# The last gate block computed inside the state-space scan

## The reference

```python
zxbcdt = einsum('bld,de->ble', h, w_in)      # z: the gate, 2048 columns
xbc = silu(conv4(xbc)); dt = softplus(dt + dt_bias); a = -exp(a_log)
def step(state, inp):                         # 2 chunks of 128 tokens, 8 groups of 4 heads
    acs = cumsum(dt_c * a, axis=1)
    decay = exp(where(causal, acs[:, :, None] - acs[:, None, :], -inf))
    cb = einsum('bign,bjgn->bijg', c_c, b_c)
    w = cb[..., None] * decay * dt_c[:, None]
    y_diag = einsum('bijgr,bjgrp->bigrp', w, x_c)
    y_off = einsum('bign,bgrpn->bigrp', c_c, state) * exp(acs)[..., None]
    new_state = ...                           # B^T (x * to_end) + decayed state
y = (y + d * x) * silu(z); y = rmsnorm(y) * gate_norm_w; out = y @ w_out
```

## Time and profile before

| what | us |
|---|---|
| median of three runs (lowest, highest) | 1849.14 (1848.16, 1850.11) |
| the profiled execution: its own time | 1850.63 |
| its span | 1849.0 |
| TensorE busy in the span | 1824.6 (99%) |
| VectorE busy | 1497.7 (81%) |
| ScalarE busy | 1267.7 (69%) |
| GpSimd busy | 118.0 (6%) |
| stretch of the last gate block and the scan | 771.03 to 825.50 |

### The profile page before, as it was taken

One profiled execution on the slowest core, in us unless ns is written; L12 is line 12 of the kernel. 1 busy time (PEld: TensorE's weight loads), 2 busy tenths in 40 slices (PEclk: granted clock), 3 DMA queues, 4 the chain that ended last, 5 costly groups with the idle time before them and its releaser, 6 DMA issues.

```text
span 1849.0 us, 27263 instructions
## 1 busy us (share of the span) xinstructions
PE 1824.6 (99%) x9312; PEld 1547.3 (84%) x9312; DVE 1497.7 (81%) x1847; ACT 1267.7 (69%) x1651; POOL 118.0 (6%) x214
## 2 busy tenths in 40 slices
PE   9999999999999999999999999999999999999997
PEld 7888788888888899888888888888888888888886
DVE  6686777777666788585898999999999999999998
ACT  5645565556544576675678778777787787777876
POOL 2040040000000000150100000000000000000100
PEclk9999999999999999999899999999999999999999
DMA  9434568563655455506799999999999999999994
GB/s 327 157 95 138 180 185 327 188 198 115 199 186 176 157 194 183 174 11 204 249 398 351 413 366 375 395 358 402 381 362 405 366 385 377 367 406 372 374 413 177
DMA packets 239355, 512.48 MB, mean 277 GB/s; under 512 B 11004, under 2 KB 58458, under 8 KB 239210
## 3 DMA queue, kind: packets, MB, share of 16 engines
q1 hardware_dynamic: 235490, 493.34, 73.4%
q0 software_dynamic: 3808, 18.38, 2.6%
HBM read 505.38 MB, written 12.07 MB: 280 GB/s over the span
## 4 chain that ended last, share of the span: by engine, by line
PE 93%; DVE 4%; ACT 1%; issue 1%; DMA 0%; ACTq 0%; SPq 0%; DVEq 0%
PE ps L261 24%; PE ps L263 24%; PE ps L262 24%; PE ps L2288 9%; PE ps L2291 4%; PE ps L2549 1%; DVE w_lo L254 1%; PE ps L2426 1%; PE ps L2129 1%; PE ps L2451 1%; ACT w_hi L245 0%; PE ps L2518 0%; PE ps L2529 0%; PE ps L2052 0%; PE ps L2344 0%
## 5 line engine op out<-in xcount | busy, mean ns | idle before, releaser
L254 DVE TENSOR_TENSOR w_lo<-raw,w_hi 128x1024 fp32r<-128x1024 f32 x938 | 1102.4, 1224 | 145.7 <-ACT w_hi L245 145.6
L245 ACT ACTIVATE w_hi<-raw 128x1024 fp32r<-128x1024 f32 x938 | 941.8, 1055 | 256.3 <-PE ps L263 241.0
L261 PE MATMUL ps<-w_hi,a 128*128 128x512 f32 (+1 forms) x1216 | 480.7, 395 | 2.1 <-DVE w_lo L1334 1.0
L263 PE MATMUL ps<-w_hi,a 128*128 128x512 f32 (+1 forms) x1216 | 472.8, 389 | 0.0
L262 PE MATMUL ps<-w_lo,a 128*128 128x512 f32 (+1 forms) x1216 | 471.8, 388 | 0.0
L261 PE MATMUL ps<-w_hi,a_hi 128*128 128x512 f32 (+1 forms) x720 | 280.4, 390 | 1.6 <-DVE a_lo L1905 1.0
L263 PE MATMUL ps<-w_hi,a_lo 128*128 128x512 f32 (+1 forms) x720 | 278.7, 387 | 0.0
L262 PE MATMUL ps<-w_lo,a_hi 128*128 128x512 f32 (+1 forms) x720 | 278.6, 387 | 0.0
L261 PEld LDWEIGHTS ps<-w_hi,a 128*128 128x128 f32 x1216 | 228.5, 188 | 49.6 <-DVE w_lo L254 1.6
L263 PEld LDWEIGHTS ps<-w_hi,a 128*128 128x128 f32 x1216 | 228.3, 188 | 48.0
L262 PEld LDWEIGHTS ps<-w_lo,a 128*128 128x128 f32 x1216 | 228.7, 188 | 44.3
(11 more groups left out here) (362 smaller groups left out, 1452.1 us busy)
## 6 DMA issues: line engine op xcount, KB each, us to landing
raw<-in_moe_w_gate_dram SPq DMA_DIRECT2D x112, 1024.0 KB, 6.9
raw<-in_moe_w_up_dram SPq DMA_DIRECT2D x112, 1024.0 KB, 7.3
raw<-in_moe_w_down_dram SPq DMA_DIRECT2D x112, 1024.0 KB, 7.1
raw<-in_ssd_w_in_dram SPq DMA_DIRECT2D x24, 1024.0 KB, 5.1
raw<-in_w_ffn_in_dram SPq DMA_DIRECT2D x22, 1024.0 KB, 5.0
raw<-in_w_in_dram SPq DMA_DIRECT2D x21, 1024.0 KB, 6.3
raw<-in_w_ffn_out_dram SPq DMA_DIRECT2D x11, 1024.0 KB, 5.0
raw<-in_dense_w_gate_dram SPq DMA_DIRECT2D x11, 1024.0 KB, 5.1
```

The source lines that it names most:

```text
L245: nc.scalar.activation(w_hi[:, u % SPL, part], raw[:, u % RAW, part], ACT.Copy).then_inc(hi_done, 1)
L254: last = nc.vector.tensor_tensor(w_lo[:, u % SPL, part], raw[:, u % RAW, part], w_hi[:, u % SPL, part].bitcast(F32), ALU.subtract)
L261: nc.tensor.matmul(o, lh, rh, start=start, stop=False, skip_group_check=True)
L263: return nc.tensor.matmul(o, ll, rh, start=False, stop=stop, skip_group_check=True)
```

## The change

Four things change.
- The broadcast of the running sums. A third small matmul gives the running sums of both halves and all heads, transposed and twice (rows 0 to 63 and again 64 to 127). VectorE rounds them, leaves the rounding's remainder in the second copy, and spreads them over four blocks, one for each head of a group (`acs_blocks`). A column of ones and zeros (`pick_group`) then picks a group in one rounded matmul of 512 columns.
- Gate block 3 is cut into eight groups of six matmuls (`gate_columns(n)`), the first before the scan's loop, the others in tiles 0 to 6, behind weights(k+2). It uses banks 5 and 6.
- Banks. Outputs of tiles 0 to 9 all use bank 4 and wait for the sum of the tile before; the state shares bank 7 with the carried part and waits for the sum of the last tile.
- Orders. weights(k+2) come before the state. z_out(3) moves behind decays(10), the split of the output unit behind decays(7) on ScalarE and ahead of sum 7 on VectorE.

```diff
@@ setup
+        acs_rows = nc.alloc_sbuf_tensor_at("acs_rows", [P, P], F32R, offset=A1_AT + 4 * 1024)
+        acs_blocks = nc.alloc_sbuf_tensor_at("acs_blocks", [P, HPG, P], F32R, offset=A1_AT + 4 * 512)
+        pick_group = nc.alloc_sbuf_tensor_at("pick_group", [P, 2 * NG], F32R, offset=A1_AT + 4 * 1152)
+        dta_twice = sm[:, 7:9, :].rearrange("p a h -> p (a h)")
+        in_group = stat[:, 8:8 + HPG]
...
-        Z_BANKS = (4, 6, 4, 6)
+        Z_BANKS = (4, 6, 4, 5)
+        ALONE = 10
+        def y_bank(k):
+            return 4 if k < ALONE else 4 + k % 2
@@ ScalarE
-                split_hi(act, O0 + 1)
-                z_out(3)
                 for k in range(2 * NG):
                     if k % 2 == 0:
                         act.wait_ge(st_s, k // 2 + 1)
-                        nc.scalar.activation(s_st, ps[6][:, 0:256].rearrange("p (r e) -> p r e", r=HPG),
+                        nc.scalar.activation(s_st, ps[7][:, 0:256].rearrange("p (r e) -> p r e", r=HPG),
                                              ACT.Copy).then_inc(st_sc, 1)
                     if k + 2 < 2 * NG:
                         decays(k + 2)
+                    if k == 5:
+                        split_hi(act, O0 + 1)
+                    if k == 8:
+                        z_out(3)
@@ VectorE, ahead of the convolution loop
+                nc.vector.tensor_copy(sm[:, 7:9, :], bcast(dta, 1, 2)).then_inc(sd_dta, 1)
...
+                nc.vector.tensor_reduce(in_group, ident.rearrange("p (k r) -> p r k", r=HPG), AX.X, ALU.add)
+                C.link(nc.vector.tensor_reduce(stat[:, 16:32], ident.rearrange("p (a k r) -> p k a r", a=2, r=HPG), AX.XY, ALU.add))
+                nc.vector.tensor_copy(pick_group[:, :], stat[:, 16:32])
@@ VectorE, behind the loop
                 dve.wait_ge(sd_acs, 1)
+                acsT = ps[7][:, P:2 * P]
+                C.link(nc.vector.tensor_copy(acs_rows[:, :], acsT))
+                C.link(nc.vector.tensor_tensor(acs_rows[64:P, :], acsT[64:P, :], acs_rows[64:P, :].bitcast(F32), ALU.subtract))
+                nc.vector.tensor_tensor(acs_blocks[:, :, :], bcast(acs_rows[:, :].bitcast(F32), 1, HPG), bcast(in_group, 2, P),
+                                        ALU.mult)
@@ VectorE, scan
-                split_lo(dve, O0 + 1)
-                dve.wait_ge(zs_done, 4)
+                dve.wait_ge(zs_done, 3)
                 for k in range(2 * NG):
+                    if k == 7:
+                        split_lo(dve, O0 + 1)
+                    if k == 12:
+                        dve.wait_ge(zs_done, 4)
@@ TensorE
-                nc.tensor.matmul(ps[7][:, 64:128], ones, dta, start=True, stop=True).then_inc(sd_acs, 1)
+                nc.tensor.matmul(ps[7][:, 64:128], ones, dta, start=True, stop=True)
+                nc.tensor.matmul(ps[7][:, P:2 * P], dta_twice, upper, start=True, stop=True).then_inc(sd_acs, 1)
...
-                    for r in range(HPG):
-                        hd = t * NH + HPG * g + r
-                        nc.tensor.matmul(ps[k % 2][:, r * P:(r + 1) * P], dta[:, hd:hd + 1].to_broadcast([P, P]), upper,
-                                         start=True, stop=True)
+                    at = NG * t + g
+                    nc.tensor.matmul(ps[k % 2][:, :], pick_group[:, at:at + 1].to_broadcast([P, P]),
+                                     acs_blocks.rearrange("p r i -> p (r i)"), start=True, stop=True)
...
                 def tile_state(g):
                     pe.wait_ge(st_xd, 3 * g + 2)
-                    nc.tensor.matmul(ps[6][:, 0:256], s_b0[:, g, :], s_xe.rearrange("p r e -> p (r e)"),
+                    if g:
+                        pe.wait_ge(st_acc, 2 * g)
+                    nc.tensor.matmul(ps[7][:, 0:256], s_b0[:, g, :], s_xe.rearrange("p r e -> p (r e)"),
...
                     pe.wait_ge(st_w, k + 1)
-                    if k >= 2:
+                    if 0 < k < ALONE:
+                        pe.wait_ge(st_acc, k)
+                    elif k:
                         pe.wait_ge(st_acc, k - 1)
+                    if k == ALONE + 1:
+                        pe.wait_ge(zs_done, 4)
...
+                def gate_columns(n):
+                    half, k = n // 4, n % 4
+                    if k == 0:
+                        pe.wait_ge(lo_done, Z0 + 6 + half + 1)
+                    cols = slice(k * WB, (k + 1) * WB)
+                    for t in range(T):
+                        last = mm3(ps[5 + t][:, :], a0_hi[:, n, t * P:(t + 1) * P], a0_lo[:, n, t * P:(t + 1) * P],
+                                   w_hi[:, (Z0 + 6 + half) % SPL, cols], w_lo[:, (Z0 + 6 + half) % SPL, cols],
+                                   n == 0, n == DC - 1)
+                    if k == 3:
+                        last.then_inc(unit_used, 1)
+
                 tile_weights(0)
                 tile_weights(1)
-                pe.wait_ge(zs_done, 2)
-                mm_rows(pe, Z0 + 6, ps[6:8])
                 pe.wait_ge(zs_done, 3)
+                gate_columns(0)
                 for k in range(2 * NG):
+                    if k + 2 < 2 * NG:
+                        tile_weights(k + 2)
+                    if k + 1 < DC:
+                        gate_columns(k + 1)
                     if k and k % 2 == 0:
                         tile_state(k // 2)
-                    if k + 2 < 2 * NG:
-                        tile_weights(k + 2)
                     tile_output(k)
                     if k == 0:
-                        pe.wait_ge(zs_done, 4)
                         tile_state(0)
```

More of the change, by code:

```diff
@@ L1695, in _ @@
                 C.link(nc.vector.scalar_tensor_tensor(dt, lgt, 0.0, lg2, ALU.max, ALU.add))
-                nc.vector.scalar_tensor_tensor(dta.rearrange("p (t h) -> p t h", t=T),
-                                               dt.rearrange("p (t h) -> p t h", t=T), -1.0, bcast(ea[:, 0:NH], 1, T),
-                                               ALU.mult, ALU.mult).then_inc(sd_dta, 1)
+                C.link(nc.vector.scalar_tensor_tensor(dta.rearrange("p (t h) -> p t h", t=T),
+                                                      dt.rearrange("p (t h) -> p t h", t=T), -1.0, bcast(ea[:, 0:NH], 1, T),
+                                                      ALU.mult, ALU.mult))
+                nc.vector.tensor_copy(sm[:, 7:9, :], bcast(dta, 1, 2)).then_inc(sd_dta, 1)
                 def block_taps(blk):
@@ L1751, in accumulate @@
                         nc.vector.tensor_tensor(before, before, bcast(eacs[:, heads], 2, HD), ALU.mult)
-                    last = nc.vector.tensor_tensor(xv, xv, ps[4 + k % 2][:, 0:256].rearrange("p (r e) -> p r e", r=HPG),
+                    last = nc.vector.tensor_tensor(xv, xv, ps[y_bank(k)][:, 0:256].rearrange("p (r e) -> p r e", r=HPG),
                                                    ALU.add)
@@ L2447, in tile_output @@
                     pe.wait_ge(st_w, k + 1)
-                    if k >= 2:
+                    if 0 < k < ALONE:
+                        pe.wait_ge(st_acc, k)
+                    elif k:
                         pe.wait_ge(st_acc, k - 1)
+                    if k == ALONE + 1:
+                        pe.wait_ge(zs_done, 4)
                     for r in range(HPG):
-                        last = nc.tensor.matmul(ps[4 + k % 2][:, r * HD:(r + 1) * HD], s_ex[k % 3][:, r, :], s_xd[k % 2][:, r, :],
+                        last = nc.tensor.matmul(ps[y_bank(k)][:, r * HD:(r + 1) * HD], s_ex[k % 3][:, r, :], s_xd[k % 2][:, r, :],
                                                 start=True, stop=True)
                     last.then_inc(st_y, 1)
+                def gate_columns(n):
[9 more added lines that the diff above has]
+                        last.then_inc(unit_used, 1)
                 tile_weights(0)
                 tile_weights(1)
-                pe.wait_ge(zs_done, 2)
-                mm_rows(pe, Z0 + 6, ps[6:8])
                 pe.wait_ge(zs_done, 3)
+                gate_columns(0)
                 for k in range(2 * NG):
+                    if k + 2 < 2 * NG:
+                        tile_weights(k + 2)
+                    if k + 1 < DC:
+                        gate_columns(k + 1)
                     if k and k % 2 == 0:
                         tile_state(k // 2)
-                    if k + 2 < 2 * NG:
-                        tile_weights(k + 2)
                     tile_output(k)
                     if k == 0:
-                        pe.wait_ge(zs_done, 4)
                         tile_state(0)
```

## The result

The changed kernel takes 1854.63 us (median of 21 runs, 1849.42 to 1863.82); the kernel before, on the same chip, 1849.14 (21 runs). By the medians it is 5.5 us slower. The ratio is 1.0035, with a 95% interval of 1.0024 to 1.0045, or 6.5 us (4.4 to 8.3). Forecast were 1852.0, in the range 1847.0 to 1856.5. So the sign was right, and the time lies in that range. It lies beyond the 0.2% that I called no change, for which I gave 0.53 (0.37 for slower than that), and beyond the 1850 to 1854 that I gave the forecast's own mechanism.

The account below looks back on a forecast made before the run. TensorE was taken to bound the scan, VectorE close behind. Tiles 0 to 6 -3.5, tiles 7 to 15 +5.1, transposed sum +0.2, slower split +0.4 and clock +0.7 gave +2.9 us: median 1852.0 us, range 1847.0 to 1856.5.

Parts of the forecast that it names:

- the forecast's own mechanism: Whole scan: gain in tiles 0 to 6, larger loss in tiles 7 to 15; 1850 to 1854 us, chance 0.52.
- The broadcast: Scan tiles: weights on TensorE fall from 1.14 to 0.45 us each, 11.0 us less TensorE work, preparation on VectorE hidden.
- TensorE's count: Rival, whole scan: TensorE's work alone sets the time, -6.8 us, 1842.3 us; chance 0.08.
- rival of a costly matmul: Rival, scan broadcast: rounded matmul costs today's price, tiles 0 to 6 take 4.6 us more, 1856.6 us; chance 0.05.
- a bank never late: Rival, tiles 7 to 15: the shared bank delays nobody, VectorE's work sets the end, -2.1 us, 1847.0; chance 0.13.
- Opening: Scan start: TensorE idles 2.4 us for z_out(2), then 1.6 us for the first exp, both released by ScalarE.
- Tiles 7 to 15: Later scan: split, sum 7, state 4, tables, exp 11 in turn; 27.8 us against 22.7, +5.1 us.
- The split beside GpSimd: Output unit's split ahead of sum 7 on VectorE: slower while GpSimd works, 0 to +0.7, taken +0.4 us.
- The tables: ScalarE around z_out(3): two loads of 1.28 us; switch drains, 2.8 us more by the skill page, left out.
- The clock: Opening and tile 8: granted clock falls after TensorE's idle time, bounds 0 and 1.5, taken +0.7 us.
- a clock of 0.50 through several tiles: Sign in the scan that the forecast is wrong: TensorE at half clock over several tiles.
- rival of the low clock: Rival, opening and thin tiles: clock stays low 10 us at each wait, 2 and 2.2 us lost, 1855.5; chance 0.22.

Follow-up runs that it names:

- block_ahead: Changed kernel with all 48 gate matmuls, the split and z_out(3) ahead of the tiles, banks and waits as changed; 1855.50 us.
- held_early2: held_early without the 26 filler transposes ahead of state 4; 1849.24 us.
- held_bank: fillers2 with the carried part in the upper half of its tile's output bank, so no state waits for the sum before; 1849.24 us.
- own_bank: Changed kernel with the carried part in the upper half of its tile's output bank, bank 7 holding the state alone; 1852.03 us.
- fillers: Changed kernel with unread transposes in TensorE's waits in the opening and ahead of states 4 and 7; 1856.09 us.
- fillers2: fillers with 18 more transposes ahead of weights 13, and 10 ahead of each of states 6 and 7; 1851.26 us.
- held_copy: fillers2 with z_out(3) as a plain copy without silu, so ScalarE loads no table inside the scan; 1850.62 us.
- early_split: Changed kernel with the output unit's split earlier: high part behind decays(5), low part ahead of sum 4; 1857.72 us.
- bcast_alone: Kernel before with only the rounded broadcast and its preparation; 1844.68 us.
- held_early: fillers2 with the split's high part behind decays(5) and its low part ahead of sum 4, all fillers kept; 1851.67 us.

## Why the prediction was right, and where it was not

**The broadcast.** A tile's weights take 0.45 us on TensorE with gate columns behind them (798.46 to 798.91), as taken, and 0.54 with the carried part behind them (801.62 to 802.16). The preparation is hidden; ahead of the convolution it is four instructions and not five, 1.07 us together. That TensorE's count doesn't govern is shown twice: alone the edit gives 4.8 of 11.0 us, and pairs stop at 4.40 us, where TensorE waits for VectorE. The rival of a costly matmul falls by these prices, that of a bank never late by the waits of about 1 us ahead of the states in block_ahead and held_early2, and by held_bank.

**Opening.** 2.22 us idle (2.4 laid out), released by ScalarE, then 0.81 instead of 1.6, since the gate columns between the two waits ran at half clock and took the difference; in own_bank's profile, where the clock held there, it is 1.31. With the clock held (fillers), output 6 ended 0.2 us from the forecast.

**Tiles 7 to 15.** The order of waits was right: split, sum 7, state 4, then both tables, then exp 11. In after the exp wait is 1.34 us instead of 2.8, with another 1.52 for an output at half clock just before; at full clock, in fillers2, VectorE waits 2.46. Pairs took 4.78. Taken for the whole change without the clock were +2.2 us; fillers2 gives +2.4. The shares, by the profiles: placing of the split 2.5 us, shared bank at least 1.3 (2.7 by own_bank), table switches at least 0.7. The last two are lower bounds, since fillers laid for the waits of fillers2 came last once the edit had shortened those waits. The three were taken away one at a time, and waits overlap, so they needn't add up. By the runs each is under 2 us, with overlapping intervals.

**The split beside GpSimd.** Taken +0.4 us, measured +0.8: 3.19 us for 2.36. GpSimd was busy throughout (803.23 to 807.39), and each half took 1.6 us, the most that a half takes in the earlier trace rows.

**The tables.** The exp started 1.30 us after the start of its load, 814.95 to 816.25, and z_out(3) 1.30 us after its own. The drain of 1.38 us per switch of the Trainium skill (ScalarE: Activation LUTs, What ACT_TABLE_LOAD costs) is not there, so it was right to leave it out. What the switches themselves cost is open above 0.7 us (held_copy).

**The clock is the term that was mis-sized.** That the time still lies in the range is due to the range's width, which the rivals gave it: without the clock the sum was right to 0.2 us. Taken was +0.7 us within 0 to 1.5; it cost 3 to 4. I sized a fall by the one at 433 us, which lost 1.9 us, and let much of it meet idle time. Laid beside fillers2, after reaches state 4 37.23 us after the scan's start instead of 35.00 and needs 24.12 from there instead of 21.88: 2.2 us in the opening and 2.2 in the thin tiles, 4.5 of scan in this execution. Five runs of after with a clock of 0.995 or 0.996 average 1850.2 us, 1.0 above the median of before, and so bear out that most of the loss goes with the clock. One of my signs of being wrong, a clock of 0.50 through several tiles, was there: it was low from 805.9 to 812.8 us and at two more places. The rival of the low clock had put 2 and 2.2 on the same two places, and its 1855.5 us is nearest to the 1854.63 measured. It was no alternative to the forecast but came on top of it: the waits are the forecast's, and the falls go away when they are filled. Its rule, that waits between short bursts throw TensorE back to its lower clock (the Trainium skill, TensorE: Matmul & The Clock Gate, HAM oscillation), agrees with fillers2, where the same places filled with other matmuls leave the clock at 1.00. I gave it 0.22 because the row of a fall that I had was a short one; the other row, 10 us at half clock with TensorE busy up to 888, was the better guide: the falls in after's scan lasted 6.9, 6.9 and 3.5 us.

**What stays open.** In which execution the clock falls, and where, differs: own_bank and early_split held it in their openings, with the same 2.21 us wait after which after lost it. So medians of kernels with uncovered waits carry a part that one profile doesn't show. A version with own bank, early split and fillers that come last nowhere was not run. An estimate from the terms above is 54.39 - 2.7 = 51.7 us of scan, before any gain from the tables; bcast_alone, with 49.73 and 4.8 us below before, is the best that was measured.

## What to carry to other kernels

When work is moved from ahead of a loop into it, look at what lay under it: here a pure stretch of matmuls had hidden a split, two table loads and the opening of a pipeline, and moving it uncovered them all. Between bcast_alone and after lie 10.3 us, 3 to 4 of them the clock and some 7 the waits. If the profile says that another engine is 0.4 us behind the bound one, take the cheap removal (the broadcast) and leave the rearrangement. And when terms of 1 to 3 us are to be told apart on TensorE's path, fill its waits first, or the granted clock moves the time more than the edit does. But lay the fillers anew for each edit: in held_early, held_copy and held_bank a filler laid for a wait that the edit had shortened came last itself and hid part of the gain. Reading the profile of each run for what came last shows it.

## What the runs showed of the hardware

- Falls of the granted clock to 0.50 (1.2 GHz) stood at or behind idle stretches of TensorE. Behind a wait of 2.22 us that ended at 774.25 (after) it was down from 775.2, and behind one of 1.88 us that ended at 810.01 (early_split) from 811.7. In after's wait of 4.09 us (804.1 to 808.19) it was down from 805.9, and in the 1.93 us wait of fillers (812.3 to 814.27) from 812.9, so that not all of that wait can be its cause. Behind the same 2.21 us in the openings of own_bank and early_split it stayed at 1.00.
- In the scans the low clock lasted from 3.4 us (own_bank, 804.6 to 808) to 13.8 us (fillers), with TensorE busy 12.0 of the 13.8:

```profile
804.60:808.00 3.40, 3.40 (x16) 3.12 (x14) 2.51 (x5) 2.20 (x7) 2.30 (x3) 0.50 0.69 276
```

- The fall at 826 us in after followed waits of 1.25 and 1.50 us, and TensorE was busy all of its 3.60 us.
- 97 extra transposes, 11.6 us of TensorE, made the kernel 3.4 us faster by the medians (1854.63 to 1851.26), 3.1 us against before in its own series.
- Behind the scan, between 871 and 897 us, every one of these profiles, of before too, has one more fall, and its length differs from execution to execution: 10.3 us in before and bcast_alone, 3.5 in after and held_early2. So whole times of two single executions can differ by microseconds that no edit made.
